# A two-block transformer kernel: where in a partition the operands that move through TensorE begin, relative to the weights

## The reference, cut to what matters

```python
# first block
h = rmsnorm(x) * (1 + scale1) + shift1          # scale, shift, gate: from silu(c) @ w_ada
proj = h @ w_in                                 # q, k, v, r of GLA, q/kv/indexer of sparse attention, two gates
ya = gla(...) @ w_branch_a ; yb = dsa(...) @ w_branch_b
x = x + gate1 * ((sigmoid(za)*ya + sigmoid(zb)*yb) @ w_out)
h2 = rmsnorm(x) * (1 + scale2) + shift2
q = h2 @ w_q                                    # 8 heads, 2 x 128
# per token and head: top 16 of 128 + 128 sub-keys -> 16 of 16384 experts, gathered rows u and v
x = x + gate2 * sum_k( gelu(h2 . u[k]) * gates[k] * v[k] )
# second block
z = rmsnorm(x) @ w_in_2 ; a = layernorm(conv31(a_val * sigmoid(a_gt))) ; s = sc_b * conv3(sc_c * sc_v)
x = x + (g_a * (silu(a) @ w_a_out) + g_b * (s @ w_b_out)) @ w_o
u = rmsnorm(x) @ w_up ; x = x + (gelu(conv3(u[:, :2816])) * u[:, 2816:]) @ w_down
x = x + sigmoid(rmsnorm(x) @ w_ple_gate) * (p @ w_ple)
out = rmsnorm(x)
```

## Time and profile before

| | us |
|---|---|
| runs | 1426.81, 1429.04, 1429.89 |
| the profiled execution's own time | 1426.29 |
| its span | 1424.5 |
| PE busy | 1261.8 (89%) |
| PEld (weight loads) busy | 949.1 (67%) |
| DVE busy | 1071.6 (75%) |
| ACT busy | 617.9 (43%) |
| chain that ended last: DMA, PE | 30%, 28% |

### The profile page before, as it was taken

How to read it: one execution, slowest core, us unless ns; L and a number is a source line. 1 busy time by engine, 2 the same in 40 slices (tenths; PEclk the granted TensorE clock), 3 DMA queues, 4 the chain that set the end, 5 groups by cost and what they waited for, 6 DMA issues and landing times.

```text
span 1424.5 us, 19698 instructions
## 1 busy us (share of the span) xinstructions
PE 1261.8 (89%) x7042; PEld 949.1 (67%) x7042; DVE 1071.6 (75%) x2161; ACT 617.9 (43%) x1268; POOL 286.4 (20%) x278
## 2 busy tenths in 40 slices
PE   4999999999998877777777777788899999999998
PEld 3999999999953323332333332333699989999998
DVE  6897657587879777777767777776698977988556
ACT  4565365547334332333333333233652254544335
POOL 1000000000445544443444344442000000000000
PEclk8999999999999999999999999999999999999999
DMA  9946525454889999999999999999744344454460
GB/s 395 369 149 242 204 93 183 173 181 170 338 338 427 426 428 427 427 428 427 426 427 427 427 427 428 428 427 427 280 176 155 133 169 165 178 183 164 165 227 32
DMA packets 55808, 416.65 MB, mean 292 GB/s; under 512 B 6049, under 2 KB 7713, under 8 KB 9394
## 3 DMA queue, kind: packets, MB, share of 16 engines
q0 software_dynamic: 36864, 268.45, 44.8%
q1 hardware_dynamic: 18544, 146.78, 28.0%
q10 hardware_dynamic: 322, 0.36, 0.1%
HBM read 414.52 MB, written 1.05 MB: 292 GB/s over the span
## 4 chain that ended last, share of the span: by engine, by line
DMA 30%; PE 28%; DVE 5%; issue 4%; ACT 2%; POOL 1%; SPq 0%; DVEq 0%; ACTq 0%; POOLq 0%
DMA ring<-in_experts,rowid 29%; PE ps L670 6%; PE ps L672 6%; PE ps L671 6%; PE ps L1012 4%; DVE ring L2091 1%; DVE h_rows L2091 1%; PE ps L1099 1%; PE ps L1098 1%; PE ps L1097 1%; DVE w_lo L1741 1%; DVE arena L1705 1%; ACT w_hi L1172 1%; DMA arena<-in_pg_w 1%; PE ps L663 0%
## 5 line engine op out<-in xcount | busy, mean ns | idle before, releaser
L1012 PE MATMUL ps<-arena 128*128 128x512 f32 x512 | 236.2, 607 | 64.8 <-ACT arena L1475 64.6
L1012 PE MATMUL ps<-ring,arena 128*128 128x512 f32 x444 | 219.4, 648 | 41.6 <-ACT arena L1475 41.5
L1012 PEld LDWEIGHTS ps<-arena 128*128 128x128 f32 x512 | 93.5, 191 | 205.8 <-ACT arena L1475 106.2
L2091 DVE CUSTOM_DVE_ANT_0 arena<-arena 128x1024 f32<-128x1024 f32 x128 | 152.0, 1225 | 99.9 <-DMA arena<-in_experts,rowid 98.0
L594 POOL DMA_INDIRECT arena<-in_experts,rowid x128 | 128.6, 1005 | 379.4 <-DVE rowid L2068 210.7
L1012 PEld LDWEIGHTS ps<-ring,arena 128*128 128x128 f32 x444 | 88.6, 206 | 170.3 <-issue 97.2
L671 PE MATMUL ps<-h_hi,w_lo 128*128 128x256 f32 x704 | 199.9, 284 | 0.0
L670 PE MATMUL ps<-h_hi,w_hi 128*128 128x256 f32 x672 | 191.7, 285 | 0.8 <-DVE xT L2366 0.5
L672 PE MATMUL ps<-h_lo,w_hi 128*128 128x256 f32 x672 | 190.2, 283 | 0.0
L1468 ACT ACTIVATE arena<-arena 128x2 f32<-128x2 f32 x126 | 25.6, 203 | 373.3 <-DVE arena L2091 373.1
L594 POOL DMA_INDIRECT ring<-in_experts,rowid x112 | 130.0, 1161 | 138.1 <-PE ps L1012 91.8
(11 more groups left out here) (366 smaller groups left out, 2569.3 us busy)
## 6 DMA issues: line engine op xcount, KB each, us to landing
ring<-in_early_w SPq DMA_DIRECT2D x47, 1024.0 KB, 4.9
arena<-in_ada_w SPq DMA_DIRECT2D x24, 1024.0 KB, 7.7
arena<-in_up_w SPq DMA_DIRECT2D x11, 2048.0 KB, 7.8
arena<-in_z_w SPq DMA_DIRECT2D x8, 2048.0 KB, 7.8
arena<-in_down_w SPq DMA_DIRECT2D x8, 1408.0 KB, 5.9
arena<-in_o_w SPq DMA_DIRECT2D x2, 2048.0 KB, 7.7
arena<-in_pg_w SPq DMA_DIRECT2D x2, 2048.0 KB, 7.7
arena<-in_experts,rowid POOLq DMA_INDIRECT x128
```

The costliest lines, as they stand in the source:

```text
L1012: mm = pe.matmul(BK[4 + 2 * t + b], diag[:, j, :], rows[j][:, D + b * 512:D + (b + 1) * 512], start=first and j == 0, stop=last and j == ( ...
L2091: v.tensor_tensor_reduce(out=u, in0=u, in1=h2tok[:, t, :], scale=1.0, scalar=0.0, op0=ALU.mult, op1=ALU.add, accum_out=dots[:, even, j:j + ...
```

## The change: what it does, and the diff

`to_line` shrinks from 24 to 8 words, 64 bytes less, so that `ident` begins at byte 17344 and every tensor behind it begins 64 bytes ahead of a multiple of 256 (192 bytes past one). `a_ring` grows by `ASIDE` = 16 words, which brings the ring (`e_hi`, `e_lo`, `w_hi`, half of the gathered rows) back to the multiple. Inside of the arena 16 words put `s_all`, the gathered rows, `diag`, the raw chunks and `w_lo`, `first_hi` back on it, and 48 more words put `comb2`/`c_lo`, `c_hi` and `f_hi` off it again. The moving operands `n`, `g`, `d`, `m`, `x2`, `h`, `c` and `f` thus begin at 192 bytes past a multiple of 256 (`x2` with 8k more), and their weights at 0. In the product `gv`, where activations are the weights, it is the other way round. The products of the expert stage keep both operands at multiples, as do those of `yb` (L663). Where both operands lie in the part that moves (attention, transposes, `ones`), both move by the same 64 bytes. No instruction is added, removed or moved: the five engines have the same instructions in the same order, apart from line numbers that are 3 higher from there on.

```diff
-        sb("to_line", [P, 24])
+        sb("to_line", [P, 8])
...
         SIZE = 28352
+        LINE, ASIDE = 64, 16
...
         a_hT = a_hh + KD * T
-        a_ring = a_hT + KD * T
-        TOTAL = a_ring + (RAW + 3) * HALF
-        arena, h_rows, ring = overlay(("arena", [P, a_hT], F32), ("h_rows", [P, KD * T], F32),
+        a_ring = a_hT + KD * T + ASIDE
+        TOTAL = a_ring + (RAW + 3) * HALF + LINE - ASIDE
+        arena, h_rows, ring = overlay(("arena", [P, a_hT], F32), ("h_rows", [P, KD * T + ASIDE], F32),
                                       ("ring", [P, TOTAL - a_ring], F32))
...
         qs = again(2 * D + 1536, 4, T + 2)
-        at[0] += 56
+        at[0] += LINE - 8 + ASIDE
         s_all = view(NT * EH + 2, 2 * NKEY)
...
-        rows = [flat_at(a_raw + j * 2 * D, 2 * D) for j in range(8)] + [flat_at(a_hT, 2 * D)]
+        rows = [flat_at(a_raw + j * 2 * D, 2 * D) for j in range(8)] + [flat_at(a_hT + ASIDE, 2 * D)]
...
         sT, scb, zg = again(a_high, CC, T), view(CC, T), view(16, T)
+        at[0] += LINE - ASIDE
         a_c = at[0]
...
-        c_lo, c_hi = alias("c_lo", a_c, KD, T), alias("c_hi", a_tail, KD, T)
-        f_hi = alias("f_hi", a_high, FB, T)
-        a_f = a_high + FB * T
+        c_lo, c_hi = alias("c_lo", a_c, KD, T), alias("c_hi", a_tail + LINE - ASIDE, KD, T)
+        a_f = a_high + LINE - ASIDE
+        f_hi = alias("f_hi", a_f, FB, T)
+        a_f += FB * T
```

## The result

The changed kernel takes 1407.48 us, the median of four runs from 1405.59 to 1408.45. The kernel before, in the same four rounds, takes 1428.61 us. The ratio is 0.9851, with a 95% interval of 0.9834 to 0.9868: 21.1 us, or 1.5%, less. In a later series the pair measured 1407.55 against 1425.58, a ratio of 0.9881 (0.9858 to 0.9904). The forecast was 1419 us in a range of 1404 to 1431; the time lies in the range, but the gain is more than twice the one that was worked out. That the time fell inside is luck in good part: the case that the forecast held for the likeliest goes down to 116.7 ns, which is 15 us off 1427, or 1412 us, and 1409 with the 3 us between the runs shown; that sum leads neither to its lower end of 1406 nor to the range's 1404.

The account below looks back on a forecast made before the run. TensorE was taken to bound everything outside the experts, DMA the expert stage. The profiled 1426.29 us less 8.9 is 1417.4, or 1420.1 by the median of runs; the forecast said 1419 us, range 1404 to 1431.

Parts of the forecast that it names:

- the case that the forecast held for the likeliest: All fp32r matmuls outside the experts: distance falls to 117 to 119 ns, times of 1406 to 1424 us; chance 0.50.
- The mechanism: Outside the experts TensorE bounds; changed low address bytes alter the 120.0 ns between matmul starts, with no instruction changed.
- 4470 matmuls at 2.0 ns, 8.9 us: Matmuls taken to count, 0.87 of 5136, each going from 120.0 to 118.0 ns: the whole predicted gain.
- the lower bound of 116.7: In product `ik`, 24 matmuls with 40 weight columns start 116.7 ns apart, taken as the shortest distance after the change.
- The second witness: In `pq`, 24 matmuls of 258 columns, moving operand 0 to 56 bytes off: 118.8 ns, 117.9 less the two columns.
- The inference from 40 columns: In `ik`, a third of the weight traffic is hardly faster, so most of the 13 ns isn't the operands' quarrel.
- The allowance for hidden matmuls: Matmuls beside other engines' chains (47 us) and at starts of stages (33 us): 80 of 616 us, 13%, bring nothing.
- The offset does nothing: Rival for all fp32r matmuls: 120 ns belong to the instruction, a fixed offset returns there; 1427 to 1430 us, chance 0.22.
- the Trainium skill's rule of independent read ports: TensorE has two independent SBUF read ports, weight loads take no bandwidth from the running matmul; time stays at 1429 us.
- removes nearly all: Rival: 64 bytes keep the operands' reads apart, distance falls towards 109 to 113 ns; 1388, perhaps 1395 us; chance 0.10.

Follow-up runs that it names:

- shift_all: Kernel before with `to_line` at 8 words: moving operands, weights, rows and chunks all 192 bytes past a multiple of 256; 1439.25 us, ratio 1.0054.
- shift128: Kernel before with everything behind the small tensors moved together to 128 bytes past a multiple of 256, `iota16` put into `vec`; 1436.21 us, ratio 1.0075.
- shift32: Kernel before with `to_line` at 16 words: everything moved together to 224 bytes past a multiple of 256; 1435.63 us, ratio 1.0072.
- weights_off: Changed kernel with `to_line` back at 24 words: moving operands on multiples of 256, weights, rows and chunks 64 bytes past; 1422.01 us, 0.9927 of the kernel before.
- f_back: Changed kernel with `f_hi` and part of `f_lo` back on multiples of 256, so 400 of 528 down-projection matmuls have relation 0; 1407.69 us.
- half_weights: Changed kernel with only 64 of 128 weight columns loaded in the up projection, from the fifth product on; 1412.72 us in one run.
- after_again: Changed kernel unaltered, run again in a later series; 1407.55 us, 0.9881 of the kernel before.
- a kick: Changed kernel with one small float32 transpose ahead of each of six products that had mostly followed the long pattern; 1412.12 us, 0.9902 of the kernel before.

## What the prediction had right, and the step that failed

**The mechanism was right.** TensorE outside of the experts is what counts, no instruction changed, and the relation of the operands sets the distance. `shift_all`, `shift128` and `shift32` (relation 0, 120.0 ns) with `weights_off` (relation -64 with the moving operands where they were, 116.5 ns) show it from both sides, and `f_back` shows it for one product alone. The first block shrank by 7.4 us and the second by 10.8, where the forecast had 4 and 5.

**The step that failed is the term "4470 matmuls at 2.0 ns, 8.9 us".** Its 118.0 ns, and the lower bound of 116.7, came from product `ik`, where the weights' offset changes with every k, so that the relation lasts for three matmuls and no one pattern can settle. With one offset kept, the distances settle at 113.33 or 117.78, and the mean over all is 115.3. The text named what it didn't know ("whether one fixed offset, repeated thousands of times, stays there") but then let the lower bound stand on rows in which the relation changes. The second witness, the block of `pq` at 118.8 ns, doesn't bear on it either: after the change such blocks take 120.6. Measured: 4.6 ns instead of 2.0. With the 4470 matmuls that were taken to count it would have been 20.6 us off 1426.29, or 1406.

**The inference from 40 columns failed.** The text read 116.7 ns with a third of the weights as a sign that "most of the 13 ns is not a quarrel between the two operands". The relation alone took 6.8 ns of 120.0 away in the up projection, and `half_weights` shows why the row misled: fewer weight columns give another distance, 119.0 ns where full loads have 113.2, so nothing about the full load follows from them.

**The allowance for hidden matmuls was somewhat small, and lay elsewhere.** Of 5136 x 4.6 = 23.6 us the profiles show 18.2, or 77%, against the 87% assumed. By itself that would have made the forecast too large, by 2.4 us of the 23.6; it hid a little of the first error. In the first block nearly all of it counts: 7.4 us gained, where the distances by operand account for about 7.5. In the second block they account for 15.4 us, and 10.8 arrive. What was given back there, from the waits of TensorE from the second block on (waited for: us in total, times, longest), before:

```profile
PE ps L670 <- DVE arena L2358: 3.0, 1, 3.0
PE ps L670 <- DVE h_lo L1705: 1.7, 1, 1.7
PE ps L670 <- DVE xT L2366: 0.5, 1, 0.5
PE ps L731 <- DVE arena L1705: 0.4, 1, 0.4
PE ps L670 <- issue: 0.3, 1, 0.3
```

and after:

```profile
PE ps L673 <- DVE arena L2361: 3.0, 1, 3.0
PE ps L673 <- DVE xT L2369: 1.6, 1, 1.6
PE ps L673 <- DVE w_lo L1744: 1.0, 1, 1.0
PE ps L734 <- DVE arena L1708: 0.8, 1, 0.8
```

The three small waits of before, 1.2 us, have become 3.4 us (the 1.7 us for `h_lo` stands in both kernels; after, it falls ahead of the stretch that the view covers). VectorE, unchanged, comes later than TensorE at these places: the split of `w_lo`, the convolution, and `xT` ahead of the last product. The other part is the clock. Behind the 3.0 us pause ahead of the `c` product the kernel after runs its first matmuls at half speed:

```profile
1165.71 0.55 PE L673 MATMUL ps<-c_hi,w_hi 128*128 128x256 f32 x1 [2.99 <-DVE arena L2361]
1166.06 0.42 PE L674 MATMUL ps<-c_hi,w_lo 128*128 128x256 f32 x1
1166.28 0.41 PE L675 MATMUL ps<-c_lo,w_hi 128*128 128x256 f32 x1
1166.49 0.41 PE L673 MATMUL ps<-c_hi,w_hi 128*128 128x256 f32 x1
...
1168.61 0.29 PE L674 MATMUL ps<-c_hi,w_lo 128*128 128x256 f32 x1
```

They start 213.3 ns apart, which is 256 columns at one per cycle of 1.2 GHz, until 1168.6; then 0.12 us. 13 starts took 2.90 us, where 13 x 0.113 = 1.47 would do: 1.4 us lost. The kernel before has the same pause, and behind it the full clock from the second start on (the third is at 1175.82):

```profile
1175.51 0.36 PE L670 MATMUL ps<-c_hi,w_hi 128*128 128x256 f32 x1 [2.99 <-DVE arena L2358]
1175.70 0.28 PE L671 MATMUL ps<-c_hi,w_lo 128*128 128x256 f32 x1
```

At the head of the second block both kernels run at 1.2 GHz, the kernel before until 1020.74 us and the kernel after until 1015.05:

```profile
1020.74 0.28 PE L671 MATMUL ps<-h_hi,w_lo 128*128 128x256 f32 x1
...
1015.05 0.28 PE L673 MATMUL ps<-h_hi,first_hi 128*128 128x256 f32 x1
```

From their first matmuls (1017.24 and 1009.85, above) that is 16 starts in 3.50 us and 24 in 5.20 us. At 120.0 and 117.8 ns they would have taken 1.6 and 2.4 us less, so the kernel after loses 0.8 us more there. Waits and clock are 2.2 + 1.4 + 0.8 = 4.4 of the 4.6 us; the last 0.2 us I didn't place. While the clock is at 1.2 GHz, the starts are 213.3 ns apart in both kernels: the relation costs or saves nothing then.

**The rest held.** The experts' part stayed (610.7 us both), no load and no VectorE work took over in the up projection, and `gv`, with the relation reversed, has 113.3 ns, the short pattern. VectorE's operands at 192 cost nothing: the dot products take 1.22 us each in both traces, the splits of `w_lo` 4.42 us. "The offset does nothing" fell: by the Trainium skill's rule of independent read ports (TensorE: Matmul & The Clock Gate, the step-by-step account) all these kernels would have had one distance. The traces have 113.2, 117.6 and 120.0 ns for the same matmuls, so the measurement decides against it as a rule for fp32r with a load in each matmul. The rival "removes nearly all" (109 to 113 ns, chance 0.10) was not far off either: the short pattern's 113.3 lies at its edge, and the mean of 115.3 between its 113 and the 117 at which the likeliest case began.

**What the plan of the prediction missed** is the second half of the change. It took the words that bring rows and chunks back to the multiple as part of the arithmetic of addresses. The three shifted kernels, 8.9, 10.8 and 10.3 us slower than the kernel before, show that they are worth some 10 us of their own: without them, `weights_off` keeps 6.5 us at 400 us and has lost all of it by 1018 us.

Two things stay open. What chooses between the 113.33 and the 117.78 pattern: the same program chose differently in a few stretches of two executions (`after_again`), and a kick flipped it without control. And why even the short one is 6.7 ns above the 106.7 ns of columns (half of the 213.3 ns measured at 1.2 GHz): neither half of the weights nor any of the six relations tried removed it. The trace shows addresses acting on the distance; what in the hardware they act on, no run shows. None of the kernels tried beat the changed one. If every product took the short pattern, it would be 2.0 ns less on 5136 matmuls, 10 us at most.

## What to carry to other kernels

Where every fp32r matmul loads its weights, as here with 256 columns, try the moving operand 64 bytes off the weights modulo 256, and keep it there for all k; then judge by the start-to-start distance in a stretch without gaps, not by the mean length of a matmul nor by the total, which can hide a few microseconds. Keep the destinations of gathered rows on multiples of 256 bytes while doing it: the one is worth about 4% of such matmuls' time, the other 1.5% of a gather. And never take a bound for a repeating stream from rows in which the relation changes after every few matmuls.

## What the runs showed of the hardware

- The distance of fp32r matmuls of 256 columns with a weight load each goes by the operands' relation modulo 256 bytes: in the up projection 120.0 ns at 0 (four different places), 118.3 at -32, 118.7 at -96 and 120.0 at 128; at -64 and at +64 a stretch has 113.3 or 117.8. Each of these is a pattern that repeats, with a period of 3 to 24 starts wherever it isn't 120.0 throughout.
- At 64 bytes there are two repeating patterns, and a stretch keeps the one it has (up to 860 starts) until a pause, another matmul or a late start comes.
- At a granted clock of 1.2 GHz the same matmuls start 213.3 ns apart with relation 0 and with -64 alike.
- Fewer weight columns (64 instead of 128) made it 119.0 instead of 113.2 ns, in one execution.
- A gather of rows of 8 KB ran at 424 to 427 GB/s with its destinations on multiples of 256 bytes, and at 420 to 422 with them 64, 128, 192 or 224 bytes past one, with the same share of busy DMA engines.
- After a pause of 3.0 us TensorE ran 2.9 us at 1.2 GHz in the kernel after and from the second start on at 2.4 GHz in the kernel before. The mean granted clock of 0.93 from 1165 to 1190 us hardly shows it.
